# Differential attention scores as rounded products over stacked halves, with the keys doubled by transfers on the chip

## What is computed

```python
s = jnp.einsum('bqhjd,bkhjd->bhjqk', qb, kb) - slopes[None, :, None, None, None] * dist
s = jnp.where(dist >= 0, s, -jnp.inf)
p = jax.nn.softmax(s, axis=-1)
a = p[:, :, 0] - lam * p[:, :, 1]
outs.append(jnp.einsum('bhqk,bkhe->bqhe', a, vb))
```

## Time and profile before

| | |
|---|---|
| median of 3 runs | 909.71 us (909.49 to 909.90) |
| the profiled execution, its own time | 908.68 us |
| its span, first to last instruction | 906.9 us |
| PE busy | 896.1 us, 99% of the span |
| DVE, ACT, POOL busy | 423.1, 397.3, 439.2 us |
| granted clock of PE | 1.000 |
| steps of the differential attention | about 320 to 516 us of the span |

### The profile page before, as it was taken

The page is one execution under the profiler, slowest core; times in us unless marked ns, Lnnn a source line. Parts: engine busy times, 40 slices in busy tenths (PEclk is TensorE's granted clock), DMA queues, the critical chain, the costliest instruction groups (busy, mean ns, idle before and its releaser), DMA issues.

```text
span 906.9 us, 12615 instructions
## 1 busy us (share of the span) xinstructions
PE 896.1 (99%) x4648; PEld 712.7 (79%) x4648; DVE 423.1 (47%) x957; ACT 397.3 (44%) x872; POOL 439.2 (48%) x376
## 2 busy tenths in 40 slices
PE   9999999999999999999999999999999998999998
PEld 7878888888888877777777788889888765777776
DVE  3221251545114413467474455646648866543631
ACT  5533323333223344454554444244435774655531
POOL 4544436445446654646444444545458382234362
PEclk9999999999999999999999999999999999999999
DMA  8442222313333332122222233233433321011113
GB/s 317 152 104 77 65 70 79 108 59 105 96 104 100 97 90 73 48 72 70 69 55 63 70 116 139 93 108 96 120 101 105 94 87 53 25 47 47 47 47 116
DMA packets 43564, 81.29 MB, mean 90 GB/s; under 512 B 4416, under 2 KB 6208, under 8 KB 43504
## 3 DMA queue, kind: packets, MB, share of 16 engines
q1 hardware_dynamic: 42016, 79.95, 29.3%
q10 hardware_dynamic: 1488, 0.55, 0.3%
HBM read 78.36 MB, written 2.12 MB: 89 GB/s over the span
## 4 chain that ended last, share of the span: by engine, by line
PE 84%; DVE 8%; issue 3%; POOL 2%; DMA 2%; ACT 1%; SPq 0%; ACTq 0%; DVEq 0%; POOLq 0%
PE Z L1708 23%; PE Z L1710 22%; PE Z L1709 22%; PE A L1885 3%; PE A L1808 2%; PE A L1923 2%; PE A L1894 2%; PE A L1820 2%; DMA raw<-in_w_in 2%; DVE z_sb L1239 1%; PE A L1868 1%; POOL w_lo L943 1%; DVE rstd L1142 1%; PE A L1833 1%; PE A L1718 1%
## 5 line engine op out<-in xcount | busy, mean ns | idle before, releaser
L943 POOL TENSOR_TENSOR w_lo<-raw,w_hi 128x512 fp32r<-128x512 f32 (+1 forms) x262 | 345.3, 1325 | 443.9 <-ACT w_hi L574 442.6
L574 ACT CAST w_hi<-raw 128x512 fp32r<-128x512 f32 (+1 forms) x262 | 157.9, 614 | 293.7 <-PE Z L1710 259.7
L1708 PE MATMUL Z<-w_hi,hT_hi 128*128 128x512 f32 (+1 forms) x544 | 217.8, 400 | 0.1
L1710 PE MATMUL Z<-w_hi,hT_lo 128*128 128x512 f32 (+1 forms) x544 | 211.3, 388 | 0.0
L1709 PE MATMUL Z<-w_lo,hT_hi 128*128 128x512 f32 (+1 forms) x544 | 210.8, 388 | 0.0
L1708 PEld LDWEIGHTS Z<-w_hi,hT_hi 128*128 128x128 f32 x544 | 102.3, 188 | 27.8 <-issue 8.3
L1710 PEld LDWEIGHTS Z<-w_hi,hT_lo 128*128 128x128 f32 x544 | 102.1, 188 | 20.8
L1709 PEld LDWEIGHTS Z<-w_lo,hT_hi 128*128 128x128 f32 x544 | 102.4, 188 | 17.7
L1708 PE MATMUL Z<-hT_hi,w_hi 128*128 128x512 f32 x260 | 113.1, 435 | 0.3 <-DVE hT_lo L1174 0.3
L1710 PE MATMUL Z<-hT_hi,w_lo 128*128 128x512 f32 x260 | 102.1, 393 | 0.0
L1709 PE MATMUL Z<-hT_lo,w_hi 128*128 128x512 f32 x260 | 101.6, 391 | 0.0
(11 more groups left out here) (239 smaller groups left out, 1298.7 us busy)
## 6 DMA issues: line engine op xcount, KB each, us to landing
raw<-in_w_in SPq DMA_DIRECT2D x91, 512.0 KB, 3.8
raw<-in_w_out SPq DMA_DIRECT2D x16, 512.0 KB, 3.6
raw<-in_ret_w_o SPq DMA_DIRECT2D x8, 512.0 KB, 3.2
raw<-in_diff_w_o SPq DMA_DIRECT2D x8, 512.0 KB, 3.3
x_sb<-in_x SPq DMA_DIRECT2D x4, 512.0 KB, 6.0
x_sb<-in_xT SPq DMA_DIRECT2D x4, 512.0 KB, 6.8
out<-x_sb SPq DMA_DIRECT2D x8, 256.0 KB, 2.9
raw<-in_w_in SPq DMA_DIRECT2D x4, 416.0 KB, 3.3
```

The source lines that it names most:

```text
L574: act.copy(w_hi[:, s % SPLIT_SLOTS, 0:width], raw[:, c % RAW_SLOTS, s - CHUNK_START[c], 0:width]).then_inc(hi_ready, 1)
L943: pool.tensor_tensor(w_lo[:, s % SPLIT_SLOTS, 0:width], raw[:, c % RAW_SLOTS, s - CHUNK_START[c], 0:width], w_hi[:, s % SPLIT_SLOTS, 0:wid ...
L1708: pe.matmul(out, l_hi, r_hi, start=first, stop=False)
L1710: return pe.matmul(out, l_lo, r_hi, start=False, stop=last)
```

## The change

The scores become two fp32r products over 128 rows in the place of one f32 product over 64. For each half j, `q_stack` holds the rounded queries of the half in its own 64 partitions and the low part (the float less the rounded) in the other 64. `keys_once` holds the high and low part of the turned keys of both halves. Four transfers for each head copy them within the on-chip memory into `k_stack`, so that both sets of 64 partitions hold the same half of the keys. A product of the stacked queries with the high keys and one with the low keys are accumulated in the same bank.

ACT writes the high queries in two instructions of 64 partitions and the high keys in one, DVE computes the low parts in three instructions straight from `A[2]`, and `turn_probs` now waits for the low part. SP issues the four transfers of 256 KB (`keys_spread`) ahead of the weights of slabs 8, 12, 20, 28, 36, 40, 44 and 48, counted from group 13, and waits for the low keys before them. The turns move from blocks i of 1 and 2 to blocks i of 0 and 1, and the keys go first except for heads 0 and 4. `diff_due` becomes flatter at first and again between v of 116 and 129, and steeper from 130. `q_stack` and `keys_once` lie in the place of `sgd_sb`, and `k_stack` in that of `qT` and `kT`. The rest of the diff, left out below, declares the semaphores and moves POOL's empty step.

```diff
--- before.py
+++ after.py
@@ -105,7 +105,7 @@
 WARM = 4
-DIFF_FIRST, DIFF_SECOND, DIFF_THIRD, DIFF_LAST = 10, 116, 160, 208
+DIFF_FIRST, DIFF_SECOND, DIFF_THIRD, DIFF_LAST = 16, 116, 130, 208
@@ -113,10 +113,22 @@
     if v < DIFF_SECOND:
-        return 36 * (v - DIFF_FIRST + 1) // (DIFF_SECOND - DIFF_FIRST)
+        return 34 * (v - DIFF_FIRST + 1) // (DIFF_SECOND - DIFF_FIRST)
     if v < DIFF_THIRD:
-        return 36 + 22 * (v - DIFF_SECOND + 1) // (DIFF_THIRD - DIFF_SECOND)
-    return min(86, 58 + 28 * (v - DIFF_THIRD + 1) // (DIFF_LAST - DIFF_THIRD))
+        return 34 + 5 * (v - DIFF_SECOND + 1) // (DIFF_THIRD - DIFF_SECOND)
+    return min(86, 39 + 47 * (v - DIFF_THIRD + 1) // (DIFF_LAST - DIFF_THIRD))
+def keys_first(w):
+    return w % 4 != 0
+def turn_count(w, i):
+    return 2 * w + 1 + (1 - i if keys_first(w) else i)
+KEYS_SPREAD = {8: 0, 12: 1, 20: 2, 28: 3, 36: 4, 40: 5, 44: 6, 48: 7}
@@ -269,10 +281,16 @@
         m_sb = sb("m_sb", [P, TT, D], F32)
+        with ExitStack() as scope:
+            keys_once = sb("keys_once", [P, 2, S], F32R, scope)
+            sb("sgd_middle", [P, 2, S], F32, scope)
+            q_stack = sb("q_stack", [P, 4, S], F32R, scope)
         sgd_sb = sb("sgd_sb", [P, KD, S], F32)
         xT = sgd_sb[:, :, :]
         mT, x2T, gateT = (v[:, :, :].rearrange("p t d -> p (t d)").rearrange("p (k s) -> p k s", k=KD)
                           for v in (m_sb, x_sb, o_sb))
+        with ExitStack() as scope:
+            k_stack = sb("k_stack", [P, 4, 2, S], F32R, scope)
...
@@ -400,6 +419,11 @@
             return A[2] if w else A[2 + i]
+        def stack_slot(w, j):
+            return 2 * (w % 2) + j
+        halves = (slice(0, DK), slice(DK, P))
@@ -492,6 +516,15 @@
                 sp.dma_start(raw[:, 0, k, :], a["w_in"][P * k:P * (k + 1), 0:512]).then_inc(raw_ready[0] if k else w_first, 16)
+            def keys_spread(w):
+                sp.wait_ge(k_lo, w + 1)
+                if w >= 2:
+                    sp.wait_ge(s_mm, 8 * (w - 1))
+                for j in range(2):
+                    for half in halves:
+                        sp.dma_start(k_stack[half, stack_slot(w, j), :, :].bitcast(F32), keys_once[halves[j], :, :].bitcast(F32)).then_inc(k_in, 16)
@@ -523,6 +556,8 @@
                     sp.wait_ge(row_out, 16)
+                if SLAB0[g] + k - SLAB0[G_DIFF0] in KEYS_SPREAD:
+                    keys_spread(KEYS_SPREAD[SLAB0[g] + k - SLAB0[G_DIFF0]])
@@ -715,14 +750,19 @@
             def diff_queries(w):
-                act.wait_ge(qk_t, 2 * w + 1)
-                act.activation(qT[:, w % 2, :], diff_qk_bank(w, 0)[:, :], ACT.Copy,
-                               scale=cols[:, 35:36]).then_inc(qk_out, 1)
+                act.wait_ge(qk_t, turn_count(w, 0))
+                if w >= 2:
+                    act.wait_ge(s_mm, 8 * (w - 1))
+                for j, half in enumerate(halves):
+                    act.activation(q_stack[half, stack_slot(w, j), :], diff_qk_bank(w, 0)[half, :], ACT.Copy,
+                                   scale=cols[half, 35:36]).then_inc(q_hi, 1)
             def diff_keys(w):
-                act.wait_ge(qk_t, 2 * w + 2)
-                act.activation(kT[:, w % 2, :], diff_qk_bank(w, 1)[:, :], ACT.Copy,
-                               scale=cols[:, 36:37]).then_inc(qk_out, 1)
+                act.wait_ge(qk_t, turn_count(w, 1))
+                if w:
+                    act.wait_ge(k_in, 64 * w)
+                act.activation(keys_once[:, 0, :], diff_qk_bank(w, 1)[:, :], ACT.Copy,
+                               scale=cols[:, 36:37]).then_inc(k_hi, 1)
@@ -736,8 +776,8 @@
                     yield
-                    if i in (1, 2) and h + 1 < H:
-                        (diff_queries if i == 1 else diff_keys)(h + 1)
+                    if i in (0, 1) and h + 1 < H:
+                        (diff_keys if keys_first(h + 1) == (i == 0) else diff_queries)(h + 1)
...
@@ -1438,12 +1478,31 @@
                     yield
-                    if i in (1, 2) and h + 1 < H:
+                    if i in (0, 1) and h + 1 < H:
                         yield
-                    yield
+                        (keys_low if keys_first(h + 1) == (i == 0) else queries_low)(h + 1)
+                    yield
+            def queries_low(w):
+                for j, half in enumerate(halves):
+                    dve.wait_ge(q_hi, 2 * w + j + 1)
+                    slot = stack_slot(w, j)
+                    dve.scalar_tensor_tensor(q_stack[halves[1 - j], slot, :], diff_qk_bank(w, 0)[half, :],
+                                             cols[half, 35:36], q_stack[half, slot, :], ALU.mult,
+                                             ALU.subtract).then_inc(q_lo, 1)
+            def keys_low(w):
+                dve.wait_ge(k_hi, w + 1)
+                dve.scalar_tensor_tensor(keys_once[:, 1, :], diff_qk_bank(w, 1)[:, :], cols[:, 36:37], keys_once[:, 0, :],
+                                         ALU.mult, ALU.subtract).then_inc(k_lo, 1)
             def diff_slot(g, k, steps, norms):
                 v = TT * (KD * (g - G_DIFF0) + k)
+                if g == G_DIFF0 and k == 1:
+                    queries_low(0)
+                    keys_low(0)
@@ -1785,8 +1844,11 @@
                 c0 = 1024 * i + P * w
-                if 4 * w - 4 + i > 0:
-                    pe.wait_ge(p_out, 4 * w - 4 + i)
+                at = turn_count(w, i) - turn_count(w, 0 if w % 4 == 0 else 1)
+                if 4 * w - 5 + at > 0:
+                    pe.wait_ge(p_out, 4 * w - 5 + at)
+                elif at and w:
+                    pe.wait_ge(k_lo, 2)
@@ -1799,14 +1861,18 @@
                     h = n // 4
-                    pe.wait_ge(qk_out, 2 * h + 2)
+                    if n % 4 == 0:
+                        pe.wait_ge(q_lo, 2 * h + 2)
+                        pe.wait_ge(k_in, 64 * (h + 1))
                     if n:
                         pe.wait_ge(s_max, 2 * n)
                     for i in (0, 1) if n % 4 == 0 else (n % 4,):
                         for j in range(2):
-                            rows = slice(DK * j, DK * (j + 1))
-                            pe.matmul(A[j][:, score_columns(i, True)], qT[rows, h % 2, P * i:P * (i + 1)],
-                                      kT[rows, h % 2, 0:P * (i + 1)], start=True, stop=True).then_inc(s_mm, 1)
+                            bank, keys = A[j][:, score_columns(i, True)], slice(0, P * (i + 1))
+                            slot = stack_slot(h, j)
+                            q = q_stack[:, slot, P * i:P * (i + 1)]
+                            pe.matmul(bank, q, k_stack[:, slot, 0, keys], start=True, stop=False)
+                            pe.matmul(bank, q, k_stack[:, slot, 1, keys], start=False, stop=True).then_inc(s_mm, 1)
@@ -1826,8 +1892,11 @@
                     job, mi = divmod(m + 1, 4)
-                    if mi in (1, 2) and job + 1 < H:
-                        pe.wait_ge(qk_out, 2 * job + 2 + mi)
+                    if mi in (0, 1) and 0 < job + 1 < H:
+                        if keys_first(job + 1) == (mi == 0):
+                            pe.wait_ge(k_lo, job + 2)
+                        else:
+                            pe.wait_ge(q_lo, 2 * job + 4)
@@ -1842,8 +1911,8 @@
                     yield
-                    if i in (1, 2) and h + 1 < H:
-                        diff_turn(h + 1, i - 1)
+                    if i in (0, 1) and h + 1 < H:
+                        diff_turn(h + 1, 1 - i if keys_first(h + 1) else i)
```

More of the change, by code:

```diff
@@ L354, in build @@
         r_xe, q_latent = sem("r_xe"), sem("q_latent")
-        qk_t, qk_out, bias_r = sem("qk_t"), sem("qk_out"), sem("bias_r")
+        qk_t, bias_r = sem("qk_t"), sem("bias_r")
+        q_hi, q_lo, k_hi, k_lo, k_in = sem("q_hi"), sem("q_lo"), sem("k_hi"), sem("k_lo"), sem("k_in")
         s_mm, s_max, s_exp, s_comb = sem("s_mm"), sem("s_max"), sem("s_exp"), sem("s_comb")
```

## The result

The changed kernel takes **916.0 us** (median; 913.8 to 916.9), the kernel before 909.8 (909.5 to 910.1). The ratio is 1.0066, 95% interval 1.0053 to 1.0079: 6 us slower, where 904.3 had been forecast and 908.8 was the upper end. A second measurement of the same two kernels gave 913.7 against 908.7, 1.0052 (1.0040 to 1.0065). The profiled execution took 916.43 us with a span of 914.6, against 908.68 and 906.9: 7.7 us of span are to be found. The second measurement has a profile too (`after_again`), with a span of 912.7, 5.8 us longer than before.

What follows compares the result with a forecast made beforehand. PE, busy 99% of the span, was taken as the bound. 908.68 − 6.5 (score blocks) − 0.9 (head 4's wait) + 2.0 (hold of `A[2]`) = 903.3 us profiled; the median lies 1.03 above, so 904.3 us, range 901.0 to 908.8.

Steps and rivals of the forecast that it cites:

- What bounds the kernel: Attention's fast stretch: PE busy all but 0.9 of 90 us, so shortening its instructions shortens the kernel unless new waits arise.
- Score blocks, −6.5 us: Attention's score products: a head falls from 3.35 to 2.54 us, eight heads from 26.8 to 20.3 us.
- The 0.40 us that was no streaming: Each of 24 old score blocks: price of going from whole-array products to pairs on halves and back, 9.6 us in all.
- Rivals B and C: Score blocks: B, narrow rounded products at full-float pace, 907.8 (0.04) or 917.7 us (0.03); C, the 0.40 us stays, 913.9 (0.05).
- Head 4's wait, −0.9: Turn of head 4's keys: PE's 0.90 us wait for the normalisation goes, between 0 and −0.9 us.
- The longer hold of `A[2]`, +2.0: Turned queries and keys: bank held longer, 0.25 us charged for each of eight turns of heads 4 to 7; 0 to 7.
- Rival A: Hold of `A[2]`: ACT or DVE late at most of eight late turns, PE waits 0.9 us each, 909.5 us; chance 0.10.
- Transfers, 0 (0 to +4): Key transfers in the attention and the weight loads behind them in SP's queue: 0 charged, 0 to +4 us kept.
- Rival D: Last four heads: loads reach ACT late, exponentials too, PE waits a microsecond in each, 908.3 us; chance 0.08.

Runs made afterwards that it cites:

- the best version: Changed kernel with ACT copying the turned bank out, low keys on POOL, a fitted schedule and 16 idle transfers more: 907.96 us, ratio 0.9996 to the kernel before.

## Why the prediction was wrong

**What bounds the kernel.** "An instruction that is made shorter there shortens the kernel by that much, as long as no new wait takes its place" was true and too easily passed over. The shares were read from one stretch of 90 us with DVE at 54%. The waits arose in groups 15 to 18, and in the first part of them DVE was busier. The same view of the kernel before, and below it of the changed one, for 55 us:

```profile
370.00:425.00 55.00, 54.10 (x276) 40.87 (x274) 37.68 (x98) 26.88 (x74) 32.25 (x32) 1.00 0.24 68
```

```profile
370.00:425.00 55.00, 50.53 (x265) 41.96 (x264) 39.84 (x101) 26.25 (x73) 31.64 (x31) 1.00 0.30 87
```

37.68 of 55 is 69%, and within it stand runs of 6 us without a gap. The window that was read began exactly where it ended.

**Score blocks, −6.5 us**: right, block by block (0.92, 0.71, 0.90 us for the 0.92, 0.70, 0.92 forecast). 128 columns cost 0.11 us (330.27 to 330.38), as in the earlier trace rows. The 0.40 us that was no streaming went with the halves. Rivals B and C fell. The Trainium skill's page "TensorE: Matmul & The Clock Gate" (Part 3: Packing small matmuls) names no cost of going between products on the whole array and pairs on its parts, only a tail for each product that increments a semaphore. As many products increment one after the change as before (64), so that tail is no part of the difference. By the Trainium skill these blocks would have become longer; by this measurement they became 0.13 to 0.35 us shorter each.

**Head 4's wait, −0.9**: 0.9 became 0.3 by the profile's rows, and the turns together −0.6.

**The longer hold of `A[2]`, +2.0: this step failed.** It was sized as latency, with "DVE and ACT free at that moment", and "in the slow first part a step takes 2.0 us and everything is covered". It measured +9.2 us in the blocks of turned probabilities (+10.4 in the second profile), outside its own bound of 7. Two of the three long waits are in the first part, at v under 116. The step looked for a single long piece of DVE in the stretch of heads 5 to 7 and not for what stands ahead of the low parts in DVE's order, which for head 3 and head 4 is a normalisation of six microseconds. And it was held to be about the hold alone. DVE's work without a hold costs 5.1 us (for somewhat more work, and at other waits); with the low parts nearly without length, 4.8 us of the 9.2 stay; and a bank that is freed at once, with DVE's order left as it is, gives nothing back. So the length of the low parts and their place in DVE's queue behind other work each make about half. How much of the second half is the hold's own, no run separates. Rival A had the right place and, with 7.2 us, nearly the right size, but was given 0.10 and the fast stretch only.

**Transfers, 0 (0 to +4): this term failed too.** It was right for the attention, where the kernel with idle transfers ran as before. It was wrong in the sum, since group 25 cost 4.4 us in one profile and 1.4 in the other, more than 160 us behind the last transfer, at a place that the forecast did not look at. In the kernel before, 32 idle transfers cost 1.1 us there. Sixteen transfers more took 0.0014, 1.3 us, off the ratio of the best version. For the changed kernel itself the profile shows the gain (no wait in group 25), while the intervals of the ratios (1.0043 for 1.0052 and 1.0066) overlap. Rival D had loads of weights as the victim inside the attention, which was not seen.

**Sum.** −6.5 + 0.8 (waits at scores) − 0.6 + 9.2 − 0.2 + 0.3 (products at a lower clock) is the attention's +3.0; with +4.4 and +0.2 it is the 7.7 us of span (0.1 by rounding). The 4.4 is the term that varies: the second profile has 4.2 + 1.4 + 0.2 = 5.8.

## What to carry to other kernels

An engine that is idle half the time on average can still be the second bound in a piece of ten microseconds. Before work is moved to it, read its timeline around each place where the new work will stand in its order, and count what is queued ahead of it, for every such place and not for the fastest stretch alone. Look beyond the changed stretch as well: part of this loss lay 160 us behind it. When a wait is removed by freeing a buffer or by reordering, and the time does not move, try both together before either is given up. A gain on the critical engine is had only if the work that pays for it is placed where nobody waits.

## What the runs showed of the hardware

**The landing of a scattered write changed with how many transfers went before.** 2 KB in 4-byte pieces landed in 9.5, 9.5, 12.0 and 9.3 us after 0, 16, 32 and 48 more transfers on another engine's queue. In the changed kernel with its own 32 the fetch behind it came after 13.7 and 12.3 us, and with 48 the write landed in 9.3. Why is open. The load of 512 KB of weights issued 4 us behind the write landed in 9.7 to 10.9 us where the others in that stretch take 3.5 to 4.8, in the kernel before as in the changed one.

**After a wait of two to three microseconds PE sometimes ran for a while at half its clock.** Timeline of PE in the changed kernel with 16 transfers more, after a wait of 2.25 us:

```profile
422.47 1.04 PE L1897 MATMUL A<-z_sb,pT 128*128 128x128 f32 x6
423.17 0.78 PE L1778 MATMUL Z<-w_hi,hT_hi 128*128 128x512 f32 x1
423.74 0.63 PE L1779 MATMUL Z<-w_lo,hT_hi 128*128 128x512 f32 x1
424.17 0.63 PE L1780 MATMUL Z<-w_hi,hT_lo 128*128 128x512 f32 x1
424.59 0.63 PE L1778 MATMUL Z<-w_hi,hT_hi 128*128 128x512 f32 x1
```

The products start 0.43 us apart instead of 0.23 (granted clock 0.50 from 423 to 426 us, the level of 1.2 GHz instead of 2.4), seven of them here: some 1.5 us on top of the wait. The same wait does not always bring it. In the first profile of the changed kernel it was 2.28 us long and the clock stayed up (1.00 from 422 to 426.5 us); in the second it was 2.25 us and the clock fell (0.63 in the same stretch). That is most of the 1.1 us by which the attention differs between the two. Behind the wait of 1.8 us at 391 the clock stayed up in both, behind that of 2.4 us at 470 it fell in both. The mean granted clock of the profiled executions was 0.996 in the changed kernel and 1.000 before.

**Some instructions of DVE are stretched beside POOL.** One of 32 columns took 1.22 us at 386.89 where its neighbours take 0.19, and a multiply of 512 columns 1.67 at 418.93 instead of 0.69. POOL's subtract ran beside each:

```profile
386.77 1.30 POOL L983 TENSOR_TENSOR w_lo<-raw,w_hi 128x512 fp32r<-128x512 f32 x1 [1.25 <-ACT w_hi L609]
...
418.73 1.32 POOL L983 TENSOR_TENSOR w_lo<-raw,w_hi 128x512 fp32r<-128x512 f32 x1 [2.12 <-ACT w_hi L609]
```

The first DVE instruction ends 0.04 us behind POOL's, the second 0.55 behind it, as if each had stood still beside it. The Trainium skill says in "GPSIMD Engine Reference" (its table of properties, row SBUF interfaces) that POOL shares its access to on-chip memory with VectorE, against instructions with two inputs there among others; both instructions are of that kind, and the rows agree. So do the low parts: one of their inputs is in PSUM, and all 24 took 0.74 to 0.76 us, seven of them begun beside a subtract. The idle ones of the run with DVE's work alone had both inputs in on-chip memory, and four of them took 1.7 to 1.8. An instruction of line 1177 with one input was stretched too (1.24 us at 415.40, its like 0.18 at 416.67, beside a subtract from 415.31 on); the same row names a second case, a mode with two ports, but nothing here tells whether it ran in that. So a multiply of the normalisation that takes 0.69 us by itself has a second price of 1.7 us, and it is paid in just those stretches where the low parts stand behind it.
